# Recurrence of a two-block model: the triangular inverse in compact tiles, its last level in quadrants, turned tiles and raw products in row halves

## The reference, cut to what matters

```python
def step(S, inp):
    w_t, k_t, v_t, kk_t, kka_t = inp[:5]
    S = (S * w_t[:, :, None, :]
         - jnp.einsum('bhij,bhj->bhi', S, kk_t)[..., None] * kka_t[:, :, None, :]
         + v_t[..., None] * k_t[:, :, None, :])
    y = jnp.einsum('bhij,bhj->bhi', S, inp[5]) if emit else None
    return S, y
```

## Time and profile before

| | |
|---|---|
| median of 3 runs | 2365.6 us (2364.36 to 2367.05) |
| profiled execution, its own time | 2363.97 us |
| its span | 2362.1 us |
| TensorE busy, matmuls | 2240.9 us, 95% |
| VectorE busy | 1454.3 us, 62% |
| ScalarE busy | 1006.6 us, 43% |
| recurrence, 850 to 1268.5 us | TensorE 387.58, VectorE 316.78, ScalarE 182.46 us busy |

### The profile page before, as it was taken

The page is one execution under the profiler, slowest core; times in us unless marked ns, Lnnn a source line. Parts: engine busy times, 40 slices in busy tenths (PEclk is TensorE's granted clock), DMA queues, the critical chain, the costliest instruction groups (busy, mean ns, idle before and its releaser), DMA issues.

```text
span 2362.1 us, 46812 instructions
## 1 busy us (share of the span) xinstructions
PE 2240.9 (95%) x20668; PEld 1845.7 (78%) x20668; DVE 1454.3 (62%) x2443; ACT 1006.6 (43%) x1768; POOL 85.4 (4%) x83
## 2 busy tenths in 40 slices
PE   8999999999999999999999999998999999899997
PEld 5864478888877788899988899896677879667786
DVE  3273536867656367887774553465475877656576
ACT  2344333332323225544442563344354655544565
POOL 1000000000010000000000001120000002000000
PEclk9999999999999999999999999998999999999999
DMA  8335237756522100000002346544355853204485
GB/s 354 107 115 207 89 138 292 263 198 240 209 95 107 36 1 3 3 4 3 12 3 105 137 179 244 214 161 179 143 200 214 334 215 142 72 1 179 172 336 185
DMA packets 47307, 348.02 MB, mean 147 GB/s; under 512 B 5264, under 2 KB 5280, under 8 KB 5760
## 3 DMA queue, kind: packets, MB, share of 16 engines
q1 hardware_dynamic: 45936, 334.52, 37.6%
q0 software_dynamic: 1168, 10.51, 1.1%
HBM read 343.96 MB, written 1.05 MB: 146 GB/s over the span
## 4 chain that ended last, share of the span: by engine, by line
PE 79%; DVE 12%; ACT 6%; issue 1%; DMA 1%; DVEq 0%; ACTq 0%
PE banks L544 27%; PE banks L2233 7%; PE banks L1032 6%; PE banks L3100 3%; PE banks L3101 3%; PE banks L3102 3%; PE banks L2092 2%; PE banks L1850 2%; PE banks L609 2%; PE banks L3131 2%; PE banks L2310 2%; PE banks L3133 2%; PE banks L3132 2%; PE banks L556 1%; PE banks L2275 1%
## 5 line engine op out<-in xcount | busy, mean ns | idle before, releaser
L522 DVE TENSOR_TENSOR mlp_w_low<-weight_slots,mlp_w_high 128x2048 fp32r<-128x2048 f32 x64 | 146.5, 2289 | 187.2 <-ACT mlp_w_high L513 187.2
L522 DVE TENSOR_TENSOR moe_w_low<-weight_slots,moe_w_high 128x2048 fp32r<-128x2048 f32 x96 | 218.2, 2289 | 62.3 <-ACT moe_w_high L513 61.5
L513 ACT ACTIVATE mlp_w_high<-weight_slots 128x2048 fp32r<-128x2048 f32 x64 | 122.2, 1910 | 180.3 <-PE banks L544 112.1
L513 ACT ACTIVATE moe_w_high<-weight_slots 128x2048 fp32r<-128x2048 f32 x96 | 182.0, 1914 | 25.9 <-PE banks L3133 19.7
L2233 PE MATMUL banks<-weight_slots,arena 64*64 64x64 f32 (+1 forms) x3648 | 147.0, 223 | 19.0 <-ACT arena L2253 13.4
L2233 PEld LDWEIGHTS banks<-weight_slots,arena 64*64 64x64 f32 x3648 | 138.9, 134 | 27.3 <-ACT arena L2253 15.3
L1032 PE MATMUL banks<-arena,weight_slots 128*128 128x256 f32 (+1 forms) x512 | 140.8, 437 | 3.0 <-DVE arena L2767 1.5
L3100 PE MATMUL banks<-moe_w_high,slots_x 128*128 128x512 f32 x320 | 130.2, 407 | 2.8 <-DVE moe_w_low L522 2.8
L1032 PEld LDWEIGHTS banks<-arena,weight_slots 128*128 128x128 f32 x512 | 97.9, 192 | 43.8 <-issue 33.6
L3101 PE MATMUL banks<-moe_w_low,slots_x 128*128 128x512 f32 x320 | 127.0, 397 | 0.0
L3102 PE MATMUL banks<-moe_w_high,slots_x 128*128 128x512 f32 x320 | 126.8, 396 | 0.0
(11 more groups left out here) (445 smaller groups left out, 5068.8 us busy)
## 6 DMA issues: line engine op xcount, KB each, us to landing
weight_slots<-weights SPq DMA_DIRECT2D x318, 1024.0 KB, 4.9
arena<-small POOLq DMA_DIRECT2D x1, 2560.0 KB, 8.9
arena<-x_t POOLq DMA_DIRECT2D x1, 2048.0 KB, 12.4
arena<-bias POOLq DMA_DIRECT2D x1, 2048.0 KB, 11.4
constants<-consts POOLq DMA_DIRECT2D x1, 1410.0 KB, 17.5
out_t<-arena SPq DMA_DIRECT2D x1, 1024.0 KB, 3.9
parameters<-params POOLq DMA_DIRECT2D x1, 763.0 KB, 21.3
arena<-pool_inv POOLq DMA_DIRECT2D x1, 512.0 KB, 14.5
```

Of the source, the lines that this page charges most:

```text
L513: nc.scalar.activation(self.pair(j)[0], slot(j, 0, SLOT), ACT.Copy).then_inc(*act.step("high", j))
L522: nc.vector.tensor_tensor(self.pair(j)[1], slot(j, 0, SLOT), self.pair(j)[0], ALU.subtract).then_inc(*v.step("used", j))
```

## The change

The inverse of levels 1 to 4 has only blocks of up to 32, so a 64x64 tile's two diagonal blocks are kept side by side in 32 columns. `X` and `XI` become `[128, 8, 32]`. For levels 1 to 4 `z` has `BM` (64 columns) as weights and `X` with 32 columns moving, and its masked copy `Z` spreads the 32 columns over 64; `grow` likewise. Transpose and copy work on 256 elements per partition. The last level is the one block off the diagonal: products of 32 rows by 32 columns, from `QUADRANT` (an unmasked copy of that block, taken with `bm`'s mask), and ScalarE copies the result out without a mask (`last_z_out`). The full inverse is put together in `INVERSE`: ScalarE writes one half's diagonal (`inverse_half`, zeroed in the other rows by a scale) after level 4, the rest after level 5. A tile is turned by 16 products with the 64x64 identity, one bank a tile, and moved out in one copy. The raw products go by row halves, 32 of them, one bank a direction. `first_inverse` folds the two blocks first (one pass more). The tables of constants change to match.

```diff
-        for i, n in enumerate(("X", "XI", "Z", "U", "GN")):
-            WK[n] = slots_area(1024 * i, 2, PAIRS, 64)
+        for i, n in enumerate(("X", "XI")):
+            WK[n] = slots_area(512 * i, 2, PAIRS, 32)
+        QUADRANT = slots_area(1024, 2, PAIRS, 32)
+        for i, n in enumerate(("Z", "INVERSE", "W")):
+            WK[n] = slots_area(1536 + 1024 * i, 2, PAIRS, 64)
         AR_OF = [WK["AR"], slots_area(5120, 2, PAIRS, 128)]
-        XI_OF = [WK["XI"], slots_area(7168, 2, PAIRS, 64)]
+        WK["GN"] = slots_area(7168, 2, PAIRS, 64)
+        WK["U"] = WK["Z"]
+        def last_z(d):
+            return WK["Z"][:, d, 0:4, :].rearrange("p a (b c) -> p (a b) c", c=32)
...
-        def pairs_turned(pe, key, src, ready=()):
-            for part in range(2):
-                b = take_bank(pe, key + (part,), WORK_BANKS)
-                for e in ready:
-                    pe.wait_ge(*after(*e))
-                for n in range(4):
-                    ins = nc.tensor.transpose(psum(b, n * P, P, slice(0, 64)), src[:, 4 * part + n, :], cn("ident"))
-                ins.then_inc(*pe.step(*key, part))
+        def strip(q):
+            return slice(32 * q, 32 * q + 32)
+        def halves_matmul(b, lhs, rhs, opens):
+            for p in range(PAIRS):
+                for h in range(2):
+                    ins = nc.tensor.matmul(psum(b, p * 32, 32, half(h)), lhs(p, half(h)), rhs(p, half(h)), start=opens,
+                                           stop=True, skip_group_check=True)
+            return ins
+        def strips_matmul(b, strips, lhs, rhs):
+            for p in range(PAIRS):
+                for q, to in strips:
+                    ins = nc.tensor.matmul(psum(b, p * 32, 32, strip(to)), lhs(p, q), rhs(p, q), start=(p == 0), stop=True,
+                                           skip_group_check=True)
+            return ins
+        OWN_TO_OTHER = [[(0, 1), (2, 3)], [(1, 0), (3, 2)]]
+        OTHER_TO_OWN = [[(1, 0), (3, 2)], [(0, 1), (2, 3)]]
+        def pairs_turned(pe, key, src):
+            b = take_bank(pe, key, WORK_BANKS)
+            I = cn("ident64")
+            for p in range(PAIRS):
+                for h in range(2):
+                    ins = nc.tensor.matmul(psum(b, p * 64, 64, half(h)), src[half(h), p, :], I[half(h), :], start=True, stop=True)
+            ins.then_inc(*pe.step(*key))
         def turned_out(act, key, dst):
-            for part in range(2):
-                act.wait_ge(*after(*key, part))
-                src = psum(bank_of(key + (part,)), 0, 512, slice(0, 64)).rearrange("p (a h i) -> p a h i", h=2, i=64)
-                for h in range(2):
-                    nc.scalar.activation(dst[half(h), 4 * part:4 * part + 4, :], src[:, :, h, :], ACT.Copy).then_inc(
-                        *act.step())
-                act.mark("taken", *key, part)
+            act.wait_ge(*after(*key))
+            nc.scalar.activation(dst, bank3(key), ACT.Copy).then_inc(*act.step("taken", *key))
...
                 for n, low, hid in (("w_raw", "w2", HW), ("a_raw", "a2", HA)):
-                    for part in range(2):
-                        b = take_bank(pe, (n, c, part), WORK_BANKS)
-                        for i in range(4):
-                            p = 4 * part + i
-                            ins = nc.tensor.matmul(psum(b, i * P, P), LOW[low][:, p * P:(p + 1) * P],
-                                                   hid[:, c].rearrange("p a b -> p (a b)"), start=True, stop=True)
-                        ins.then_inc(*pe.step(n, c, part))
+                    b = [take_bank(pe, (n, c, d), WORK_BANKS) for d in range(2)]
+                    for p in range(PAIRS):
+                        for d in range(2):
+                            ins = nc.tensor.matmul(psum(b[d], p * CHUNK, CHUNK), LOW[low][half(d), p * P:(p + 1) * P],
+                                                   hid[half(d), c, d, :], start=True, stop=True)
+                            if p == PAIRS - 1:
+                                ins.then_inc(*pe.step(n, c, d))
...
+            def level(c, d, lv):
+                b = take_bank(pe, ("z", c, d, lv), WORK_BANKS)
+                X_, BM, BQ = WK["X"][:, d], bm_of(c, d), QUADRANT[:, d]
+                pe.wait_ge(*after("bm_out", c, d))
+                pe.wait_ge(*after("inverse", c, d, lv - 1))
+                if lv < LEVELS - 1:
+                    ins = halves_matmul(b, lambda p, r: BM[r, p, 0:64], lambda p, r: X_[r, p, :], True)
+                else:
+                    ins = strips_matmul(b, OWN_TO_OTHER[d], lambda p, q: BQ[strip(q), p, :], lambda p, q: X_[strip(q), p, :])
+                ins.then_inc(*pe.step("z", c, d, lv))
...
+                if lv < LEVELS - 1:
+                    ins = halves_matmul(b, lambda p, r: Z[r, p, :], lambda p, r: XI[r, p, :], False)
+                else:
+                    ins = strips_matmul(b, OTHER_TO_OWN[d], lambda p, q: ZQ[strip(q), p, :], lambda p, q: XI[strip(q), p, :])
...
+                    XI, W = WK["INVERSE"][:, d], WK["W"][:, d]
                     pairs_matmul(pe, ("u", c, d), lambda p, r: [(XI[r, p, :], W[r, p, :])],
-                                 ready=[("w_out", c, d), ("inverse_t", c, d, LEVELS - 1)])
+                                 ready=[("w_out", c, d), ("inverse_half", c, d), ("inverse_t", c, d, LEVELS - 1)])
...
-                    *act.step("inverse_t", c, d, lv))
+                src = psum(INVERSE_BANKS[d], 0, 256)
+                if lv < LEVELS - 1:
+                    nc.scalar.activation(flat(WK["XI"][:, d]), src, ACT.Copy).then_inc(*act.step("inverse_t", c, d, lv))
+                else:
+                    nc.scalar.activation(WK["INVERSE"][:, d, :, 32 * (1 - d):32 * (1 - d) + 32],
+                                         src.rearrange("p (a b) -> p a b", b=32), ACT.Copy).then_inc(
+                        *act.step("inverse_t", c, d, lv))
+            def last_z_out(c, d):
+                act.wait_ge(*after("z", c, d, LEVELS - 1))
+                nc.scalar.activation(last_z(d), psum(bank_of(("z", c, d, LEVELS - 1)), 0, 256).rearrange(
+                    "p (a b) -> p a b", b=32), ACT.Copy).then_inc(*act.step("taken", "z", c, d, LEVELS - 1))
+                act.mark("z_out", c, d, LEVELS - 1)
+            def inverse_half(c, d):
+                act.wait_ge(*act.own)
+                nc.scalar.activation(WK["INVERSE"][:, d, :, 32 * d:32 * d + 32], WK["XI"][:, d], ACT.Copy,
+                                     scale=cn("own_rows", d, 1)).then_inc(*act.step("inverse_half", c, d))
...
+                    if lv == LEVELS - 1:
+                        for d in range(2):
+                            last_z_out(c, d)
                     for d in range(2):
                         inverse_out(c, d, lv)
                     if lv in (1, 4):
-                        system_out("w", "U", c, 0 if lv == 1 else 1)
+                        system_out("w", "W", c, 0 if lv == 1 else 1)
+                    if lv == LEVELS - 2:
+                        for d in range(2):
+                            inverse_half(c, d)
...
-                    bias_ = pr(bias_name).rearrange("p (d a) -> p a d", d=2)
-                    for part in range(2):
-                        own = slice(4 * part, 4 * part + 4)
-                        v.wait_ge(*after(n + "_raw", c, part))
-                        tt(buf[:, :, own, :].rearrange("p d a i -> p a d i"),
-                           psum(bank_of((n + "_raw", c, part))).rearrange("p (a d i) -> p a d i", d=2, i=CHUNK),
-                           bias_[:, own, :].unsqueeze(3).to_broadcast([P, 4, 2, CHUNK]), add).then_inc(
-                               *v.step("taken", n + "_raw", c, part))
+                    for d in range(2):
+                        v.wait_ge(*after(n + "_raw", c, d))
+                        tt(buf[:, d], bank3((n + "_raw", c, d)), over_steps(bias_name, d), add).then_inc(
+                            *v.step("taken", n + "_raw", c, d))
...
-                    tt(dst[:, pairs[0]:pairs[0] + n, 0:w], src, mask, mul).then_inc(*v.step("taken", name, c, d, i))
+                    src = psum(bank_of((name, c, d, i)), 0, n * g * 64).rearrange("p (a g b) -> p a g b", g=g, b=64)
+                    if name == "bm":
+                        nc.vector.tensor_copy(QUADRANT[:, d, pairs[0]:pairs[0] + n, :],
+                                              src[:, :, 0, 32 * (1 - d):32 * (1 - d) + 32]).then_inc(*v.step())
+                    tt(dst[:, pairs[0]:pairs[0] + n, 0:g * 64].rearrange("p a (g b) -> p a g b", b=64), src,
+                       mask.unsqueeze(1).to_broadcast([P, n, g, 64]), mul).then_inc(*v.step("taken", name, c, d, i))
...
+                XI, bm = WK["XI"][:, d], bm_of(c, d)
+                I = cn("ident32").unsqueeze(1).to_broadcast([P, PAIRS, 32])
+                first = cn("first_level", 32 * (1 - d), 32).unsqueeze(1).to_broadcast([P, PAIRS, 32])
+                if c:
```

(24 more changed lines are left out.)

51 lines of the change are left out of this document (21 added, 30 removed).

## The result

The changed kernel takes **2352.8 us** (median of 5 runs, 2347.1 to 2353.4) against 2365.6 us (5 runs, 2363.9 to 2370.4) for the kernel before: a ratio of 0.9945, with a 95% interval of 0.9934 to 0.9955. The forecast was 2353.0. The profiled execution took 2352.81 us, its span 2350.9; that of before 2363.97 and 2362.1. So the profiled difference is 11.2 us, 12.8 by the medians.

What follows compares the result with a forecast made beforehand. TensorE's records plus its waits were taken to bound the recurrence. Bank waits, transposes, last level, strips, raw products and seed (-0.9) summed to -30.7 us; clock falls gave back +18, net -12.7 from 2365.6: 2353 us, range 2330 to 2378.

Steps and rivals of the forecast that it cites:

- Bank waits, -13.4: Turned tiles: one bank a tile instead of two ends TensorE's waits for ScalarE's copies, -13.4 us.
- Compact levels, 0: Levels 1 to 4: weights stay 64 columns, so halving the moving columns to 32 gains TensorE 0.
- transposes, -2.6: VectorE's transposes shrink from 512 to 256 elements, shortening TensorE's waits before level 3 and the last level, -2.6 us.
- Rival 2: Levels 1 to 4: the moving side sets the pace, compact records at 15.6 ns; 2308 us, chance 0.07.
- Last level, z to grow: Last level: ScalarE's copy chain of 2.6 us sets when grow starts, instead of 3.21 us after z; -5.0 us.
- Strips at 15.6 ns: Last level: two 32-row strips run at once at 15.6 ns a record, grow products saving -7.8 us.
- Rival 4: Last level: strips run one at a time, 31 ns a record, clock as forecast; 2361 us, chance 0.06.
- Raw products in row halves, -1.0: Raw products: 32 records at 115 ns become 64 at 55.4 (3.68 us to 3.55), -1 us.
- The clock, +18: Around the last level, light products drop the clock in seven chunks, 1.5 stretches each costing 1.7 us: +18 us.
- rival 1: Recurrence: no fall of the clock, -30 us, 2335 us; chance 0.25.
- rival 3: Compact levels: the clock falls there too, raw products in row halves streaming as little; +15 us, 2380 us, chance 0.17.

Runs made afterwards that it cites:

- e1: The kernel before with only the turned tiles changed: transposed by row halves into one bank per operand, moved out in two copies; 2349.1 us.
- e2: The changed kernel with the raw products as in the kernel before, all 128 rows of weights instead of row halves; 2345.8 us.
- e4: The changed kernel with ScalarE's two copies of half of the inverse moved behind its last-level z copies; 2342.1 us.
- e9: The changed kernel with both edits, e2's full-row raw products and e4's later half copies; 2333.1 us.
- e8: e9 with one direction of the next chunk's beta product put between the last level's z and grow products; 2332.3 us.
- e10: e4 with the last level's grow products issued twice, the second set writing the same values; 2365.3 us.

## Why the forecast held, step by step

The time was right to 0.2 us, and that closeness is luck: two errors cancelled. Without the falls the change was worth some 33 us, not 30.7, and the clock took 22, not 18. The runs of the kernel spread over 6 us, and the choice of 1.5 stretches for each of seven chunks was a guess.

- **Bank waits, -13.4:** right, and shown with the turned tiles alone. The step said "I count none" of the changes between tile sizes at about 0.1 us each, and counted a wait at its idle time; e1's gain of 15.8 leaves 2.4 us, which either would explain.
- **Compact levels, 0, and transposes, -2.6:** both right. Groups stay 1.9 us apart, with 32 or 64 moving columns, and the waits for transposes went from 5.6 to 3.0 us. Rival 2 is out.
- **Last level, z to grow 2.6 us instead of 3.21:** the releaser (ScalarE) and the wait (0.9 to 1.4 us) were right, the size a little small: 2.14 us in chunks 1 and 2, 2.50 in the others, which is -5.7 instead of -5.0.
- **Strips at 15.6 ns:** 14.8, and 27 if they don't alternate. Rival 4 is out. The Trainium skill's floor of about 25 ns between starts ("TensorE: Matmul & The Clock Gate", section "Wait — 56ns, not 53.3ns?"), by which the term was -2.4, is not borne out with two strips at a time; it fits the 27 ns of one strip.
- **Raw products in row halves, -1.0:** this step failed. The records gained 0.05 us in 3.84, and the falls beside them cost 6.8 us in the profiled execution; e2 puts the whole part at +7.0. The forecast took a cost for the records and none for the clock, although its third rival named these products, and it likened light streaming to the products of 60 moving columns that kept the clock. A row nearer in its rows, though lighter in its columns, stood in the same trace. The 64-row products at 2027.04 in the earlier trace rows, from which it took their price, have 15 moving columns and run 3.75 us; behind them, in the kernel before, the clock was down:

```profile
2030.00:2035.00 5.00, 2.37 (x25) 1.67 (x24) 3.99 (x11) 2.03 (x8) 0.00 (x0) 0.58 0.01 3
```

The fall began at 2030.8, before the wait of 2.10 us that follows. The prediction read this price and not this clock.

- **The clock, +18:** 22. Behind the last levels it was 23.9 us of half clock, 12 us of time, in place of 18, and in level 1 of chunk 7 another 3.4 us of time; the raw products brought the other 6.8, and they were not in the sum. The place was right: a fall came behind six last levels, where the forecast had seven.
- **Rivals 1 and 3:** the falls came (against rival 1), and hardly any within the compact levels (against rival 3): one, in chunk 7, and e4 has the same products and the same wait there without a fall.

## What to carry to other kernels

Cutting a product into smaller tiles saved TensorE time here only where the larger of weight columns and moving columns shrank (29.2 ns a record with 64 and 64 or 64 and 32, 14.8 with 32 and 32), and it cost the clock: 22 us, in falls that stood behind the small products. Look in the trace of before for the clock behind every product of a shape like the new one, not only for its price. Look for what the change does to banks and to the order of copies first; here the smaller turned tiles (one bank instead of two) were worth at least as much as the whole change, and two copies moved behind the ones that are waited for gave another 10.7 us.

## What the runs showed of the hardware beyond that

Runs of short records uncover pauses of TensorE that have no releaser in the trace ("issue"): none in the kernel before and in the changed one (where a wait stands in the same place), none with strips at 27 ns, 2.4 us in e4, 1.4 in e9, 2.5 in e8, 6.0 in e10, single ones up to 1.47 us. The groups around the longest have all of their records in the trace (168 + 24 in e10, 50 + 14 in e8), so the pauses are not gaps of the trace. The supply of instructions is the likely cause, argued and not shown. The DMA view, queue 8, of the changed kernel from 850 to 1256 us, then of e10 from 990 to 1005 (packets, MB, share of 16 engines):

```profile
q8 instruction: 86, 1.41, 1.5%
```

```profile
q8 instruction: 4, 0.07, 2.2%
```

If this queue feeds TensorE alone, which the view does not say, 1.41 MB for 21,827 matmuls and weight loads is 65 bytes each, and a packet of 16.4 KB feeds some 128 records, each with its load: one in 3.7 us at 29.2 ns a record, but one in 1.9 us at 14.8. No run varied the fetching itself, so this stays open.
